# Hybrid attention/mLSTM step: TensorE's stream written as counted loops, and the token rows cut 104/100/100 instead of 112/96/96

## The reference

```python
h = rmsnorm(x, norm_gain)                 # x: 16 meta tokens + 256 prompt frames; 32 sample frames
p = h @ w_in                              # 4096 -> all branch inputs and both gates, one projection
# MLA:    cq -> rmsnorm -> @ w_q_up;  ckv -> rmsnorm -> @ w_kv_up;  rotary key;  softmax attention, 16 heads
# mLSTM:  4 heads, dqk 256, dv 512, recurrence in chunkwise-parallel form with carried state
a = attn * silu(z_A)
m = sigmoid(o) * rmsnorm(h_mlstm) * silu(z_B)
y = x + concat([a, m]) @ w_out            # 4096 -> 4096
# outputs: y, the new latents and rotary keys, the new mLSTM states, for prompt and sample
```

## Time and profile before

| | before |
|---|---|
| median of 3 runs | 2142.31 us (2141.85 to 2142.33) |
| the profiled execution: its time | 2141.85 us |
| the profiled execution: its span | 2140.3 us |
| PE busy | 2092.7 us (98%) |
| DVE, ACT, POOL busy | 49%, 42%, 10% |
| mean granted TensorE clock | 0.995 |
| HBM traffic over the span | 149 GB/s |

### The profile page before, as it was taken

One profiled execution on the slowest core, in us unless ns is written; L12 is line 12 of the kernel. 1 busy time (PEld: TensorE's weight loads), 2 busy tenths in 40 slices (PEclk: granted clock), 3 DMA queues, 4 the chain that ended last, 5 costly groups with the idle time before them and its releaser, 6 DMA issues.

```text
span 2140.3 us, 39993 instructions
## 1 busy us (share of the span) xinstructions
PE 2092.7 (98%) x15062; PEld 2032.8 (95%) x15062; DVE 1046.5 (49%) x1868; ACT 892.7 (42%) x1751; POOL 218.7 (10%) x292
## 2 busy tenths in 40 slices
PE   4999999999999999999999999999999999999997
PEld 3999999999999899998999999999999999999997
DVE  3544565655544444443444444444445654444443
ACT  4533454545443333333333444444444543333332
POOL 1000123333200000000000000000000100000000
PEclk9999999999999999999999999999999999999999
DMA  7555443232455454543545555555555555555553
GB/s 194 151 164 159 121 120 94 87 105 80 119 146 164 119 163 122 157 142 116 177 121 154 163 166 167 167 164 164 166 167 167 159 180 187 181 180 181 187 188 106
DMA packets 189969, 321.80 MB, mean 150 GB/s; under 512 B 20524, under 2 KB 65680, under 8 KB 189424
## 3 DMA queue, kind: packets, MB, share of 16 engines
q1 hardware_dynamic: 182464, 296.92, 47.1%
q0 software_dynamic: 5488, 15.11, 2.1%
q10 hardware_dynamic: 1872, 7.60, 1.4%
HBM read 309.96 MB, written 9.62 MB: 149 GB/s over the span
## 4 chain that ended last, share of the span: by engine, by line
PE 97%; DMA 1%; ACT 0%; DVE 0%; ACTq 0%; POOL 0%; issue 0%; POOLq 0%; DVEq 0%; SPq 0%
PE bank L1297 29%; PE bank L1300 28%; PE bank L1301 28%; DMA xt<-in_x_prompt_dram 1%; PE bank L1693 1%; PE bank L1656 1%; PE bank L1545 1%; PE bank L1442 1%; PE bank L1443 1%; PE bank L1440 1%; PE bank L1457 1%; PE bank L1499 1%; PE bank L1510 1%; PE bank L1511 1%; PE bank L1745 0%; PE bank L1323 0%
## 5 line engine op out<-in xcount | busy, mean ns | idle before, releaser
L857 DVE TENSOR_TENSOR wlo<-raw,whi 128x512 fp32r<-128x512 f32 (+1 forms) x1256 | 823.2, 664 | 988.7 <-ACT whi L490 985.0
L490 ACT CAST whi<-raw 128x512 fp32r<-128x512 f32 (+1 forms) x1256 | 712.9, 577 | 1084.8 <-PE bank L1301 1044.3
L1297 PE MATMUL bank<-xhi,whi 128*128 128x288 f32 (+2 forms) x3104 | 938.0, 302 | 1.2 <-DVE wlo L857 1.1
L1301 PE MATMUL bank<-xhi,wlo 128*128 128x288 f32 (+2 forms) x3104 | 926.9, 299 | 0.0
L1300 PE MATMUL bank<-xlo,whi 128*128 128x288 f32 (+2 forms) x3104 | 925.8, 298 | 0.0
L1297 PEld LDWEIGHTS bank<-xhi,whi 128*128 128x128 f32 (+1 forms) x3104 | 586.7, 189 | 4.4 <-DVE wlo L857 1.4
L1300 PEld LDWEIGHTS bank<-xlo,whi 128*128 128x128 f32 (+1 forms) x3104 | 587.0, 189 | 1.9 <-issue 1.1
L1301 PEld LDWEIGHTS bank<-xhi,wlo 128*128 128x128 f32 (+1 forms) x3104 | 585.6, 189 | 0.0
L1297 PE MATMUL bank<-mhi,whi 128*128 128x288 f32 x1024 | 303.9, 297 | 0.0
L1300 PE MATMUL bank<-mlo,whi 128*128 128x288 f32 x1024 | 302.5, 295 | 0.0
L1301 PE MATMUL bank<-mhi,wlo 128*128 128x288 f32 x1024 | 302.5, 295 | 0.0
(11 more groups left out here) (314 smaller groups left out, 1378.6 us busy)
## 6 DMA issues: line engine op xcount, KB each, us to landing
raw<-in_w_in_dram SPq DMA_DIRECT2D x316, 512.0 KB, 3.8
raw<-in_w_out_dram SPq DMA_DIRECT2D x128, 512.0 KB, 3.7
raw<-in_w_in_dram SPq DMA_DIRECT2D x140, 256.0 KB, 2.9
raw<-in_w_q_up_dram SPq DMA_DIRECT2D x48, 384.0 KB, 3.2
raw<-in_w_kv_up_dram SPq DMA_DIRECT2D x16, 512.0 KB, 3.6
xres<-in_x_prompt_dram POOLq DMA_DIRECT2D x16, 256.0 KB, 4.9
out_dram<-ytok POOLq DMA_DIRECT2D x16, 256.0 KB, 3.0
C<-in_state_C_dram POOLq DMA_DIRECT2D x4, 512.0 KB, 4.3
```

The costliest lines, as they stand in the source:

```text
L490: ins = nc.scalar.copy(hi, src)
L857: ins = tt(lo, src, hi.bitcast(f32), ALU.subtract)
L1297: ins = mm(out, w_hi, m_hi, start=start, stop=False, **kw)
L1301: return mm(out, w_lo, m_hi, start=False, stop=stop, **kw)
```

## The change

Two things are changed. The rows of tokens are cut 104, 100 and 100 over the three tiles instead of 112, 96 and 96, and the loads that ACT issues follow: 68 and 32 rows, 16 and 88 rows, and twice 100 half rows. And five Python loops of PE's stream become counted loops; their bodies are the same calls with a register in place of the number, so that what a wait compares with is worked out from the register. Where PE's code asks whether the number of a pair is a Python integer (`q_units`), it no longer is one in the seven steps, and the wait on `cq_lo` ahead of each unit is left out there.

```diff
-X_TOK = [(0, 112), (112, 96), (208, 96)]
+X_TOK = [(0, 104), (104, 100), (204, 100)]
...
-            act.dma_start(xt[2][0:64, :], x_prompt[0, 192:256, :]).then_inc(xrow_in[2], 16)
-            act.dma_start(xt[2][64:96, :], x_sample[0, :, :]).then_inc(xrow_in[2], 16)
+            act.dma_start(xt[2][0:68, :], x_prompt[0, 188:256, :]).then_inc(xrow_in[2], 16)
+            act.dma_start(xt[2][68:100, :], x_sample[0, :, :]).then_inc(xrow_in[2], 16)
             act.dma_start(xt[0][0:N_META, :], meta).then_inc(xrow_in[0], 16)
-            act.dma_start(xt[0][N_META:112, :], x_prompt[0, 0:96, :]).then_inc(xrow_in[0], 16)
+            act.dma_start(xt[0][N_META:104, :], x_prompt[0, 0:88, :]).then_inc(xrow_in[0], 16)
             for half, t in enumerate((1, 3)):
-                act.dma_start(xt[1][0:96, XH[half]], x_prompt[0, 96:192, XH[half]]).then_inc(xrow_in[t], 16)
+                act.dma_start(xt[1][0:100, XH[half]], x_prompt[0, 88:188, XH[half]]).then_inc(xrow_in[t], 16)
...
-            for i in range(1, 3):
+            with pe.Fori(1, 3) as i:
                 group(i * KT, "cq", 0, i, N_META)
...
-            for j in range(0, 7):
+            with pe.Fori(0, 7) as j:
                 q_units(j + 1, "step", j, attention("step", j, j))
                 kv_units(j + 1, "step", j, attention("step", j, j))
...
-            for h in range(0, 3):
+            with pe.Fori(0, 3) as h:
                 group(U_ML + 2 * KT + h * (2 * KT), "ml", 0, h, 0, mlstm("ml", h, h), queries=2)
                 group(U_ML + 3 * KT + h * (2 * KT), "ml", 1, h, 0)
...
-            for g in range(0, 5):
+            with pe.Fori(0, 5) as g:
                 group(U_GATE + KT + g * (2 * KT), "gates", 0, g, N_META, b0=4)
                 group(U_GATE + 2 * KT + g * (2 * KT), "gates", 0, g, N_META)
...
-            for g in range(0, 7):
+            with pe.Fori(0, 7) as g:
                 group(U_OUT + KT + g * KT, "out", 0, g, N_META,
                       lambda k: y_rows("out", g) if k == 2 else None, a_hi=mhi, a_lo=mlo)
```

## The result

The changed kernel takes 2194.84 us (median of 4 runs, 2193.24 to 2196.82), the kernel before 2142.08 us (4 runs): a ratio of 1.0251, 95% interval 1.0233 to 1.0269. That is 52.8 us slower. I had forecast 2159 us, 17 us slower. The predicted direction is right; the time lies 10 us above the range of 2145 to 2185 us, and on the figure of rival B.

The account below looks back on a forecast made before the run. The prediction took PE, busy 98% of the span, to bound the kernel. From 2141.85 us it added 15.2 for the later start and 2 for the loops, giving 2159 us, with an 8-in-10 range of 2145 to 2185 us.

Parts of the forecast that it names:

- rival B: PE's loops: jumps back stall, each of 19 turns costing PE 2 us, 2195 us in all; chance 0.20.
- What bounds the kernel: Whole kernel: PE is busy 98% of the span, so only its start and holes between its instructions can move time.
- Part 1: Token loads at the start: equal shares on fewer engines make the last half land 15 us later.
- the ends of 36.9 and 53.0: Landing of the last token load, in us: lower end at a less crowded engine's price, upper at the price of before.
- Rival A: Token loads: spread raggedly over all 16 engines, only 2.5 us more, 2146.4 us with the loops; chance 0.13.
- Part 2: PE's five counted loops: register work hidden by the sequencer's lead, 0.1 us a turn, 2 us in all.
- The bound of 3.8 us without cover: PE's loop turns: upper end for a jump waiting on its code block, 19 x 3.8 = 72 us.
- the unknown is the code: PE's jumps back: one may have to wait for its block of 256 instructions, at a price no earlier row shows.
- The cover of 3.4 us: Output group's end: the sequencer is through at 1807.9 us but waits until 1811.3 anyway, which hides a turn's cost.
- Rival C: PE's stream is smoother as a loop, returning up to 16 us of holes, 2128 us; chance 0.05.
- The 16 us that were to bound the gain: PE's holes after its start at 31.3 us, 2140.3 - 31.3 - 2092.7, as limit for gain from dropped waits.
- Own range of the likeliest case: Forecast case's total, 2151 to 2171 us: 9 to 25 us for the start, 0 to 4 for the loops; chance 0.62.

Follow-up runs that it names:

- rows_split: Kernel before with rows cut 104/100/100, each load of 68, 88 and 100 rows split into 64, 80 or 96 rows plus the rest: 2147.57 us, ratio 1.0032.
- loops_small: Kernel before with only the short-bodied loops of PE (cq, steps, output) as counted loops: 2140.71 us, ratio 0.9998.
- gates_slot0: Kernel before with all five PE loops, rows unchanged, and the gate loop's first instruction at place 0 of its block of 256: 2148.38 us, ratio 1.0036.
- gates_slot176: Kernel before with all five PE loops, rows unchanged, and the gate loop's first instruction at place 176 of its block of 256: 2148.77 us, ratio 1.0037.
- loops_big: Kernel before with only the two long-bodied PE loops (mLSTM heads and gates) as counted loops: 2148.30 us, ratio 1.0034.
- rows_only: Kernel before with only the rows of tokens cut 104/100/100 and ACT's loads to match, PE's stream written out: 2156.77 us, ratio 1.0072.

## Why the prediction was wrong

**What bounds the kernel: right, with one thing missing.** The prediction let two things move the time, PE's start and holes between its instructions. They are most of the cost, but the clock behind the holes is a third. Of the loss at the start nothing came back.

**Part 1, equal shares on fewer engines: right in mechanism, a little small.** The landing came at 45.7 us against the 43.0 taken and the ends of 36.9 and 53.0; PE's start slipped by 18.6 us against 15. The term that was mis-sized is the price of a row on an engine: over the 28 whole and 20 half rows it comes to (45.7 - 3.1)/38 = 1.12 us a row, not 1.05. Packets of 16 KB still took 1.1 to 1.7 us on average up to 32 us, and 0.6 to 0.7 only after that. The first weights add the rest, 4.74 us to land instead of 4.04. ACT could begin the first tile's sums only at 31.07 instead of 11.44 us, and PE waited 8.4 us for scaled tokens where before it waited 2.3, but the chain runs through the last landing. Rival A, at 30 us for the landing, is excluded by this row and by rows_split. The queue of these loads shows the shares themselves. In the first 60 us it carries 471 packets (DMA view of that stretch), 404 of data in 16 and 8 KB and 67 small ones that report completion: 4 + 16 + 16 + 11 + 10 + 10, one for each engine used by each load.

```profile
q10 hardware_dynamic: 471, 4.98, 37.6%
```

That is what the Trainium skill, DMA: Bandwidth & Descriptors, section "Why a DMA increments its semaphore by 16 and not by 1", would have: the largest divisor up to 16, of 68, 32, 16, 88, 100 and 100 rows. The trace agrees as far as a sum can tell: by the same rule there are 6 x 16 = 96 small packets before and 116 in rows_split, and both traces have that many.

**Part 2, "0.1 us a turn, 2 us in all": this step failed.** Three things in it were wrong, and each has its run.

*The 19 turns were treated alike.* The bound of 3.8 us without cover was nearly the price of a jump (3.3 to 4.8 us), but it falls due at six jumps only, those of the mLSTM heads and, by the place of its head, the gates. The other 13 cost nothing (loops_small, and the gates too in gates_slot0, gates_slot176 and loops_big). I had set 1,542 and 1,756 instructions against blocks of 256 and put this down to "the unknown is the code", without asking how many blocks can be held. The counts were short, too, because they had only matmuls and weight loads: with the sequencer's own instructions the bodies are 1,609 and 1,855, and the shortest is 548, not 800.

*The cover of 3.4 us was that of another stage.* It was read at the boundary of an output group, whose body is held anyway. At the turn of the gates the sequencer reaches the jump at 1271.34 and the last matmul issued before it starts at 1273.46: 2.1 us of cover, not 3.4. Then it waits for a second block. The hole is 3.8 - 2.1 for the jump and about 3.2 us for the second wait, 4.9 together, as the timeline shows.

*The clock.* The prediction named 1.2 GHz behind the holes as a sign of rival B, but no case had a price for it. It costs 8.5 us net, a quarter of what the loops cost: behind the six jumps it is about 12 us (34.7 less 22.8 of holes), and 3.2 come back where slow stretches of before are missing.

**Rival B (0.20) named what happened and the total, but by another sum.** It had 19 turns of 2 us, 38 us; it was six turns of 3.9 us and 8.5 us of clock, 32 us, and a start 3.6 us dearer than forecast. That the totals agree within 1 us is luck: its loops were 6 us too dear, its start 3 to 4 us too cheap, and the median lies 2.6 us above the profiled execution. The Trainium skill, Runtime: NRT & Kernel Launch, section "Instruction fetch mechanics", says that a taken branch outside the current window of two pages stalls. Direction and mechanism agree with the six jumps, the window doesn't: bodies of 548, 803 and 834 instructions, up to four blocks, and 1609 in loops_big jump back in 0.21 to 0.25 us without a fetch. Another figure on that page, 2048 instructions for PE, is eight blocks. With that the runs agree: seven were held without a hint and eight with one.

**Rival C (smoother stream): nothing of it.** loops_small, without holes, comes to 0.9998 (0.9988 to 1.0007). The 16 us that were to bound the gain were misread, too: PE's last matmul ends at 2128.4 us, 11.9 before the span does, so that the holes after its start come to under 5 us.

**Own range of the likeliest case, 2151 to 2171,** would have held the start; it had no room for a jump that stalls, because the loops' upper end was cut from 72 to 4 us on the cover alone.

## What to carry to other kernels

Before a long written-out stream is made into a loop, count the body's instructions on that engine, its place in its block of 256 included, and keep it under what the instruction memory holds; here PE jumped back free of cost up to 1785 places and lost 3 to 6.5 us a turn from 1809 on. Read the cover of a stall at the very place where it will fall, not at a similar boundary of another stage, and give the clock after a hole a price of its own. Look at how a load's rows divide over the 16 engines before you look at its bytes: here 64 rows ran on 16 engines and 68 on 4.

## What the runs showed of the hardware that was not expected

- PE's sequencer holds a loop of up to seven blocks of 256 instructions (1785 places held, 1809 not). With a hint in each turn a body that lies over eight (1610 instructions from place 200) was held as well, and for a longer one (1855) the wait fell from 4.5 and 4.8 us to 2.6 and 3.1.
- A jump that misses, without a hint, costs 3.3 to 5.4 us on the sequencer; one that is held 0.21 to 0.25 us, one not taken 0.08.
- Instruction blocks fetched for PE: 119 before and 104 after, 102 in loops_big (its mLSTM body is still fetched), and 68 in gates_slot0. They count which bodies are held without a look at the timeline.
- The stretches at 1.2 GHz in the mLSTM stage vary from kernel to kernel with the same instructions, from one of 3.4 us (rows_only, loops_small) to four (before). One that is missing gave back 0.8 to 1.3 us, not the 1.7 that half speed over 3.4 us would make; three fewer are why rows_only lost 16.1 us and not 18.7.
- Three transposes of 128, 128 and 48 token rows in a unit made it 2.20 us long, of 112, 96 and 96 rows 1.89 us; why is open.
